# Cached samples' values as the moving operand in four 32-column groups, and the windows' masks added by VectorE

## What is computed

```
def _masked_softmax_stats(s, mask):            # the prompt's windows
    s = jnp.where(mask, s, -jnp.inf)
    mx = jnp.max(s, axis=-1, keepdims=True)
    p = jnp.exp(s - mx)
    l = jnp.sum(p, axis=-1, keepdims=True)
    return p / l, (mx + jnp.log(l))[..., 0]

def _mem_attention(q, mk, mv):                 # samples: mk, mv from a cache of 256 rows
    s = jnp.einsum('bthd,bnhd->bhtn', q, mk).astype(jnp.float32) * (q.shape[-1] ** -0.5)
    p = jax.nn.softmax(s, axis=-1).astype(mv.dtype)
    return jnp.einsum('bhtn,bnhd->bthd', p, mv)
...
    # _dilated_decode: samples in the windows, 128 cached rows per window and the new one
    o = jnp.einsum('bhtm,btmhd->bthd', pr.astype(vg.dtype), vg)
```

## Time and profile before

| | |
|---|---|
| median of 3 runs | 1800.95 us (1800.6, 1800.95, 1802.29) |
| the profiled execution, its own time | 1802.63 us |
| its span, first to last instruction | 1800.8 us |
| PE busy | 1770.0 us, 98% of the span |
| DVE, ACT, POOL busy | 845.1, 617.1, 460.2 us |
| share of PE in the chain that ended last | 91% |

### The profile page before, as it was taken

How to read it: one execution, slowest core, us unless ns; L and a number is a source line. 1 busy time by engine, 2 the same in 40 slices (tenths; PEclk the granted TensorE clock), 3 DMA queues, 4 the chain that set the end, 5 groups by cost and what they waited for, 6 DMA issues and landing times.

```text
span 1800.8 us, 22353 instructions
## 1 busy us (share of the span) xinstructions
PE 1770.0 (98%) x8336; PEld 1398.3 (78%) x8347; DVE 845.1 (47%) x1648; ACT 617.1 (34%) x1501; POOL 460.2 (26%) x509
## 2 busy tenths in 40 slices
PE   8999999999999999999999999999999999999998
PEld 4577765988888888658568888888888888789573
DVE  0444423785666556451341543355335534766613
ACT  1421234553655244211312124323332334743311
POOL 0151100335322012400003452155226532223000
PEclk9999999999999999999999999999999999999999
DMA  7311112145664144620111112213221434744412
GB/s 265 133 59 65 65 50 60 48 160 167 199 182 158 59 134 139 210 101 36 72 57 47 47 36 84 71 62 103 75 88 63 147 115 150 259 127 147 157 66 95
DMA packets 148806, 196.22 MB, mean 109 GB/s; under 512 B 19067, under 2 KB 107899, under 8 KB 148562
## 3 DMA queue, kind: packets, MB, share of 16 engines
q1 hardware_dynamic: 140580, 174.65, 30.6%
q10 hardware_dynamic: 8118, 20.14, 3.0%
HBM read 156.97 MB, written 37.85 MB: 108 GB/s over the span
## 4 chain that ended last, share of the span: by engine, by line
PE 91%; DVE 5%; ACT 2%; issue 1%; DMA 0%; ACTq 0%; DVEq 0%; SPq 0%
PE PS L3139 49%; PE PS L2183 11%; PE PS L2227 4%; PE PS L1982 3%; PE PS L371 3%; PE PS L535 3%; PE PS L286 2%; PE PS L2019 2%; PE PS L1994 2%; PE PS L2016 1%; PE PS L897 1%; DVE WK L704 1%; PE PS L890 1%; PE PS L1820 1%; PE PS L1311 1%
## 5 line engine op out<-in xcount | busy, mean ns | idle before, releaser
L3139 PE MATMUL PS<-HT,RING 128*128 128x258 f32 (+2 forms) x1776 | 444.3, 381 | 2.5 <-ACT WK L3229 2.1
L3139 PEld LDWEIGHTS PS<-HT,RING 128*128 128x128 f32 x1776 | 329.5, 190 | 47.8 <-ACT WK L3229 2.9
L3229 ACT ACTIVATE BIG<-PS 128x256 f32<-128x256 f32 (+2 forms) x140 | 53.8, 384 | 363.5 <-PE PS L3139 363.1
L3139 PE MATMUL PS<-BIG,RING 128*128 128x258 f32 (+1 forms) x656 | 161.4, 385 | 1.3 <-DVE BIG L3323 1.3
L2183 PE MATMUL PS<-BIG 128*128 128x512 f32 x328 | 147.3, 596 | 0.5 <-DVE BIG L3334 0.5
L3139 PEld LDWEIGHTS PS<-BIG,RING 128*128 128x128 f32 x656 | 124.0, 192 | 19.8 <-DVE BIG L3323 2.1
L3139 PE MATMUL PS<-BIG,WK 128*128 128x258 f32 (+1 forms) x448 | 112.4, 382 | 1.0 <-DVE BIG L3323 1.0
L2183 PEld LDWEIGHTS PS<-BIG 128*128 128x128 f32 x328 | 60.5, 190 | 68.0 <-issue 66.9
L3139 PE MATMUL PS<-HT,CST 128*128 128x256 f32 (+2 forms) x432 | 110.4, 383 | 0.5 <-DVE BIG L3328 0.4
L2037 ACT ACTIVATE WK<-PS,WK 128x256 f32<-128x256 f32 (+1 forms) x128 | 53.9, 426 | 152.8 <-DVE WK L2055 152.8
L3139 PEld LDWEIGHTS PS<-BIG,WK 128*128 128x128 f32 x448 | 83.4, 190 | 13.3 <-DVE BIG L3323 1.4
(11 more groups left out here) (388 smaller groups left out, 3156.0 us busy)
## 6 DMA issues: line engine op xcount, KB each, us to landing
RING<-in_w_in_a SPq DMA_DIRECT2D x14, 1024.0 KB, 6.1
WK<-in_cache_mem_kv SPq DMA_DIRECT2D x56, 256.0 KB, 5.6
RING<-in_w_kv_b SPq DMA_DIRECT2D x12, 1024.0 KB, 5.2
RING<-in_w_in_b SPq DMA_DIRECT2D x12, 1024.0 KB, 5.2
WK<-in_cache_win SPq DMA_DIRECT2D x40, 256.0 KB, 4.6
RING<-in_w_mkv SPq DMA_DIRECT2D x16, 512.0 KB, 4.7
BIG<-in_x_prompt SPq DMA_DIRECT2D x16, 512.0 KB, 3.3
BIG<-sample_query SPq DMA_DIRECT2D x28, 256.0 KB, 5.8
```

Source lines behind the costliest of these rows:

```text
L3139: last = nc.tensor.matmul(PS[:, bank, 0:mid - lo], weight_block(u // 2, s, k), h_block(layer_of(u), u % 2, t, k), start=(k == 0 and j not ...
L3229: nc.scalar.activation(part(u, n2 if j == 0 else n1, lo, mid), PS[:, banks(u)[0], 0:mid - lo], ACT.Copy).then_inc(sig("projections_copied" ...
```

## The change

Three things are changed.

1. The sample values. The weighted values are now the moving operand (128 columns a head), and the stationary one is a 128x32 piece of `PICK`, a table that is 1 in its column 7 and 0 elsewhere; the piece that begins at column 7-b has its ones in column b. The four heads go to the four groups of 32 partitions of bank 7, columns 384 to 511, and the eight batches add up there. Then ACT copies the 128x128 result (`sample_out_act`), PE transposes it (`sample_out_pe`), and DVE reads the transposed columns. In B the last two batches come one or two places earlier. POOL makes `PICK` at the start.
2. The masks. PE's mask matmul goes. DVE takes, for each of the two heads, one pass that adds the mask, negates, writes to `PROB` and keeps the minimum (which is the negated maximum); ACT's exponential reads `PROB` in place of PSUM with a scale of -1. The waits for `probs_turned`, for the stored rows and for the cast masks move from ACT and PE to DVE; PE's next scores wait for the maximum in place of the probabilities.
3. Two semaphores are merged (`scratch_saved`), and `HSS` has a place of its own.

```
         def sample_out_dve(dve, name, finish):
-            dve.wait_ge(sig("sample_out_done").sem, SMP[name]["order"] + 1)
-            finish(PS[:, 7, 0:HP])
+            dve.wait_ge(sig("sample_out_done").sem, 2 * SMP[name]["order"] + 2)
+            finish(PS[:, 7, 256:384].rearrange("p (h x) -> p h x", h=H)[:, :, 0:NS])
+
+        def sample_out_act(act, name):
+
+            act.wait_ge(sig("sample_out_done").sem, 2 * SMP[name]["order"] + 1)
+            nc.scalar.activation(SMP[name]["m"]["row"][:, 0:P], PS[:, 7, 384:512],
+                                 ACT.Copy).then_inc(sig("sample_out_copied").up(), 1)
+
+        def sample_out_pe(pe, name):
+
+            pe.wait_ge(sig("sample_out_copied").sem, SMP[name]["order"] + 1)
+            nc.tensor.transpose(PS[:, 7, 256:384], SMP[name]["m"]["row"][:, 0:P],
+                                ident).then_inc(sig("sample_out_done").up(), 1)
...
             v = value_tiles(name, b)
             for h in range(H):
-                last = nc.tensor.matmul(PS[:, 7, h * NS + b:h * NS + b + 1], v[0][:, h * P:(h + 1) * P],
-                                        ones[:, 0:1], start=(b == 0 and h == 0), stop=True,
+                last = nc.tensor.matmul(PS[32 * h:32 * (h + 1), 7, 384:512], PICK[:, 7 - b:39 - b],
+                                        v[0][:, h * P:(h + 1) * P], start=(b == 0), stop=True,
                                         skip_group_check=True)
...
                 if s >= 2:
-                    pe.wait_ge(*count("probs_ready", u - 1))
+                    pe.wait_ge(*count("probs_ready" if g in MEM else "max_ready", u - 1))
...
-                if g not in MEM:
-                    nc.tensor.matmul(bank[:, 0:2 * nk], BFC[:, M_ID:M_ID + P], mask_of(g, i),
-                                     start=True, stop=False, skip_group_check=True)
...
                 for x in range(2):
-                    last = nc.scalar.activation(PROB[:, u % 2, x * nk:(x + 1) * nk],
-                                                PS[:, 3 + u % 2, x * nk:(x + 1) * nk], ACT.Exp,
-                                                bias=negmax[:, x:x + 1], accum_out=total[:, x:x + 1])
+                    p = PROB[:, u % 2, x * nk:(x + 1) * nk]
+                    last = nc.scalar.activation(p, PS[:, 3 + u % 2, x * nk:(x + 1) * nk] if g in MEM else p, ACT.Exp,
+                                                bias=negmax[:, x:x + 1], scale=1.0 if g in MEM else -1.0,
+                                                accum_out=total[:, x:x + 1])
...
+                else:
+                    if s >= 2:
+                        dve.wait_ge(*count("probs_turned", u - 1))
...
+                    mask = mask_of(g, i)
+                    for x in range(2):
+                        at = slice(x * nk, (x + 1) * nk)
+                        last = nc.vector.tensor_tensor_reduce(PROB[:, u % 2, at], PS[:, 3 + u % 2, at], mask, -1.0, 3e38,
+                                                              ALU.add, ALU.min, negmax[:, x:x + 1])
+                    last.then_inc(sig("max_ready").up(), 1)
```

More of the change, by code:

```diff
@@ L1981, in step_pe @@
                         big(k_tile(h), (i + 1) * P - nk, (i + 1) * P)
-                    last = nc.tensor.matmul(bank[:, x * nk:(x + 1) * nk], q, k, start=(g in MEM), stop=True,
-                                            skip_group_check=True)
+                    last = nc.tensor.matmul(bank[:, x * nk:(x + 1) * nk], q, k, start=True, stop=True)
                 last.then_inc(sig("scores_ready").up(), 1)
@@ L3412, in windows_out @@
                 t = m["qk"][:, HP:2 * HP]
-                do(nc.vector.tensor_copy(y, ps))
+                do(nc.vector.tensor_copy(y.rearrange("p (h b) -> p h b", h=H), ps))
                 for g in range(3):
```

60 lines of the change are left out of this document (39 added, 21 removed).

## The result

| | before | changed |
|---|---|---|
| median | 1801.11 us (4 runs, 1800.6 to 1802.29) | 1784.99 us (4 runs, 1784.77 to 1785.6) |
| profiled execution, its own time | 1802.63 us | 1785.21 us |
| its span | 1800.8 us | 1783.4 us |

The change makes the kernel 16.1 us faster; the ratio is 0.991, with a 95% interval from 0.9893 to 0.9927. The forecast was 1786.0 us, with a range from 1783 to 1793. The forecast gain of 15.0 us lies between the two.

The account below looks back on a forecast made before the run. PE was taken to bound the kernel. Masks −7.6, third-window waits +0.4, value batches −8.5, D +0.35 and transposes +0.33 gave −15.0 us, from the median 1800.95 to 1786.0 us, range 1783 to 1793.

Parts of the forecast that it names:

- What bounds the kernel: Whole program: PE bounds, busy 1770.0 of 1800.8 us; an edit is worth what it takes off PE's list.
- The masks: Windows: 48 mask matmuls off PE save 7.6 us; waits in the third window give back 0.4 (bounds 0 and 1.5).
- A batch: Sample values: four groups work at once, so 0.54 us in place of 0.89; 24 batches save 8.4 to 8.5 us.
- Transposes and ACT's copies: Sample values in A, D and B: three added PE transposes cost 0.33 us; ACT's copies and DVE's reading cost nothing.
- D: Sample values behind the windows: both 1.38 us waits stay; the first batch's gain, 0.35 us, is lost (bounds 0 and 2).
- The clock: Half clock for 3.40 us in D cost the profiled execution 1.7 us; half or more of the executions lack it.
- Three groups or two at a time: Sample values: partial overlap; three give 1787.5 us, inside the 0.72 forecast; two give 1793.5, sharing 0.16 with DVE or POOL bounding.
- no overlap: Sample values: groups do not overlap at 128 columns, a batch takes 1.21 us, total 1801.5 us; chance 0.04.
- a drain at each group: Sample values: each record to another group drains PE, a batch takes 1.8 us, total 1817 us; chance 0.03.
- the first two windows turn to DVE: DVE or POOL replaces PE as bound in windows or D: about 1791 us; chance 0.16 together with two groups at a time.
- (d): Sample values: slower kernel, PE drained at each group change, 22.8 us more against 6.9 less: 1817 us; chance 0.03.
- (c): Sample values: no overlap of groups, 7.7 us more, masks' gain just used up: 1801.5 us; chance 0.04.

Follow-up runs that it names:

- pairs: Changed kernel with the sample-value batches of A and B taken two at a time: 1784.06 us, against 1786.59 us for the changed kernel in that series.
- fours: Four batches at a time in A and B, against a kernel with pairs, later key reduces and PE summing D's third tile for five batches: 1787.88 us.

## Why the prediction held, step by step

**What bounds the kernel.** Right. What came off PE's list came off the time.

**The masks.** 7.6 us off and 0.4 back were forecast; the windows became 7.2 us shorter. The 0.4 stood as a wait at the very step that had the smallest reserve, and the later run with the key reduces moved showed that POOL's product, and not the pass, makes it. Its reason held too: POOL's pace does not follow PE. Its size is not fixed, though: 0.45, 1.10, 0.77 and 0.43 us in four profiles whose windows are the same.

**A batch.** 0.54 us was forecast and 0.56 measured, the old one 0.90 in place of 0.89. The term was read from a run of 144 records and held for eight. With 0.34 gained a batch and not 0.35, the 24 batches give 8.2 us in place of 8.5. The 0.02 is a first cluster that lasts a little longer (0.134 us to the second in place of 0.107). All four groups work side by side: the rate of 2.38 that the Trainium skill gives for three groups (page "TensorE: Matmul & The Clock Gate", Part 3), by which a batch would take an estimated 0.60 (0.22 × 3 / 2.38 + 0.32), is not borne out here. That a change of tiling drains TensorE, as its page "TensorEngine Tiling (Array Packing)" says under Key Properties, agrees with the 0.34 us in and out.

**Transposes and ACT's copies.** No wait for them, as forecast. From the first out projection to the windows the changed kernel is 2.6 us shorter, which is eight batches at 0.34 and one transpose of 0.11.

**D.** This step failed in its detail. The forecast had both waits of 1.38 us shift along and stay, and lost 0.35 on the first batch. One stayed. The other went, and 0.4 more at the first sum and, in the first profile, 0.7 at a later one came in its place. At these places PE lost 3.6 us from start to start before and 3.2 after; smaller losses of 0.23 and 0.26 us that were not there before (at 1575.2 and 1584.9) take that back. So the waits' sum stayed, and D's 4.3 are eight batches, one transpose and 1.7 us of clock. In the second profiles the three places cost 2.9 before and 2.5 changed, as the wait of 1.38 was 0.5 there already in the kernel before. The reason given, that a run of DVE which starts on a product of PE moves along with PE, holds for the wait that stayed. For the other a likely reason is that a wait that comes earlier in DVE's run gives DVE time back; no run shows it. The sum was off by less than 0.5 us.

**The clock.** This term stays open. I took the 1.7 us at half clock to be absent from the median of before, as they were the distance of its profiled execution to the median. They stand in both profiles of the kernel before and in neither of the changed one, so between the profiled executions the gain from the first to the last out projection is 1036.0 − 1019.5 = 16.5 us. That some executions lack them is right: 17 of 45 list a mean clock of 1.0. Half or more, as I assumed, is not shown, and so it is not shown either how much of the 1.7 us the median of before contains. Measured from the 17, whose median is 1800.0, the forecast of 15.0 us less would be 1785.0; the eight executions of the changed kernel have a median of 1786.0.

**The beginning.** The same view by windows, of the kernel before and of the changed one, shows the first 512-column matmuls:

```profile
9.60:12.60 3.00, 3.00 (x6) 1.31 (x5) 0.00 (x0) 0.69 (x2) 0.00 (x0) 1.00 1.03 414
```

```profile
9.60:12.60 3.00, 3.00 (x10) 1.66 (x9) 0.00 (x0) 1.04 (x2) 0.00 (x0) 1.00 1.03 415
```

Six records in 3 us against ten: the first three stand 0.85 us apart and not 0.43, 1.2 us in all. PE's first matmuls, in order of time, before and changed:

```profile
6.24 3.67 PE L358 MATMUL PS<-CST,BIG 128*128 128x128 f32 x16 [6.24 <-DMA BIG<-in_mem_prompt]
```

```profile
6.58 3.68 PE L362 MATMUL PS<-CST,BIG 128*128 128x128 f32 x16 [6.58 <-DMA BIG<-in_mem_prompt]
```

These sixteen stand 0.21 us apart in both, where 128 columns take 0.11 elsewhere. So every execution looked at starts at half pace, and what differs is when that ends and when the first load lands. The granted clock of 1.00 in the view above cannot be held against this. The trace's first entry of the clock, at full, stands at 12.15 us before and at 10.17 changed, within a record of where the pace doubles, and the view counts time without an entry as full. In the second profiles the entry stands at 11.78 and 12.09 us and the first matmul at 7.11 and 6.24, so both come and go in both kernels, and they explain a part of why the medians of one kernel differ by 1.6 us between series. That the forecast of 1786.0 came so close is in part luck: up to 1.7 us of clock missing from the gain and 0.3 too many for the batches, against a beginning that varies by more.

**The rivals.** Three groups or two at a time, no overlap, and a drain at each group are all excluded by the batches' 0.56 us. Two groups would have been 0.87. That the first two windows turn to DVE is excluded by the 26 us that DVE took on with no wait there; in the third only the step named lost more. In two rivals a sum had slipped. A batch of 1.8 us is 0.91 more than one of 0.89, so (d) is 21.8 us and about 1816, and (c) comes to 1801.8; neither changes a chance.

## What to carry to other kernels

When an operation changes its form, look for another place of the same program that already has this form, and read from start to start what one costs and what entering and leaving costs: here that gave 0.54 for a measured 0.56. Visits to a different tiling cost 0.34 us each, so small pieces are better taken together, until the tiles that they hold are missing for the next loads (pairs gained 2.5 us, fours lost 6.9 against pairs). Where an engine off the path waits for a third one, its queue hands that wait on to everything behind it; moving one instruction there took a wait of 0.45 to 1.1 us away and brought one of 0.4 elsewhere. A wait or a stretch of low clock seen in one profile may be missing in the next of the same kernel, so look at a second one before an edit is credited with it.

## What the runs showed of the hardware

ACT's exponential takes 394 ns for 128 columns from SBUF and 500 for 256, against 362 and 469 from PSUM. DVE's pass that adds, takes the minimum and writes takes 422 ns for 256 columns of PSUM and bf16 masks of SBUF, against 406 for SBUF alone on 32 partitions at L1096. Two passes overlap: the second starts 0.35 us after the first, together with the first one's accumulator read. The program's first matmuls stand at twice their later distance (0.21 and 0.11 us for 128 columns, 0.85 and 0.43 for 512) up to the trace's first entry of the full clock, 10.2 to 12.2 us from the start in the four profiles of the two kernels. A stretch of 3.4 us at half clock behind waits of 1.4 us comes in some executions of a kernel and not in others; what decides it is open.
